# Rows of x ahead of a halved weight unit, half of the first values on another engine, scales in two bank pairs, two router rows shared by GpSimd and ScalarE

## The reference

```python
for i in range(DEPTH):                      # 2
    hn = rms_norm(h, norm_mix[i])
    if i % N_MIXERS == 0:                   # [B|C|h] = hn @ w_in; (B * conv3(C * h)) @ w_out
        h = h + short_conv_mixer(hn, conv_w_in[j], conv_w[j], conv_w_out[j])
    else:                                   # 3 head groups, (window, dilation) = (128,1), (512,4), (2048,16)
        h = h + dilated_attention_mixer(hn, attn_w_qkv[j], attn_w_o[j], cos, sin)
    hn = rms_norm(h, norm_ffn[i])           # top-1 of 4 groups, then top-2 of its 4 experts
    h = h + hierarchical_moe(hn, ...)       # silu(t @ w_gate[e]) * (t @ w_up[e]) @ w_down[e]
return rms_norm(h, norm_final)
```

## Time and profile before

| what | us |
| --- | --- |
| median of 3 runs (range) | 1403.17 (1402.56 to 1404.1) |
| the profiled execution | 1403.41 |
| its span, first to last instruction | 1401.6 |
| TensorE products busy | 1341.8 (96%) |
| VectorE busy | 1119.0 (80%) |
| ScalarE busy | 768.2 (55%) |
| GpSimd busy | 202.0 (14%) |

### The profile page before, as it was taken

One profiled execution on the slowest core, in us unless ns is written; L12 is line 12 of the kernel. 1 busy time (PEld: TensorE's weight loads), 2 busy tenths in 40 slices (PEclk: granted clock), 3 DMA queues, 4 the chain that ended last, 5 costly groups with the idle time before them and its releaser, 6 DMA issues.

```text
span 1401.6 us, 20107 instructions
## 1 busy us (share of the span) xinstructions
PE 1341.8 (96%) x6967; PEld 1104.2 (79%) x6967; DVE 1119.0 (80%) x1442; ACT 768.2 (55%) x946; POOL 202.0 (14%) x309
## 2 busy tenths in 40 slices
PE   7999988999999999999999999999997899999995
PEld 5888876888888877888888778888776788888883
DVE  6656368999999995994978768687967899999998
ACT  5222245888888856223357242224824588888882
POOL 3000021111111300221200111111002011111131
PEclk9999997999999999999999999999998899999998
DMA  5238417999999975232210222331035799999984
GB/s 211 91 121 309 188 61 260 359 389 390 392 397 388 379 268 176 83 121 90 90 61 2 99 97 92 106 103 61 2 122 207 261 378 387 392 382 394 388 341 180
DMA packets 85377, 308.92 MB, mean 220 GB/s; under 512 B 12177, under 2 KB 12201, under 8 KB 68932
## 3 DMA queue, kind: packets, MB, share of 16 engines
q1 hardware_dynamic: 75936, 291.19, 56.1%
q0 software_dynamic: 8640, 15.86, 3.0%
q10 hardware_dynamic: 740, 1.07, 0.2%
HBM read 291.72 MB, written 31.98 MB: 231 GB/s over the span
## 4 chain that ended last, share of the span: by engine, by line
PE 86%; DVE 7%; issue 3%; ACT 2%; DMA 1%; SPq 0%; DVEq 0%; POOLq 0%; ACTq 0%; POOL 0%
PE ps L329 26%; PE ps L331 25%; PE ps L330 25%; PE ps L1910 2%; PE ps L1695 2%; PE ps L1893 1%; DVE probT L1474 1%; PE ps L1590 1%; DVE h L1253 1%; PE ps L1875 1%; ACT v_all L927 1%; DVE rope_b L1541 1%; DMA x_rows<-hn_rows,tok_col 1%; DVE W_lo L978 1%; PE ps L1878 1%
## 5 line engine op out<-in xcount | busy, mean ns | idle before, releaser
L1179 DVE TENSOR_TENSOR W_lo<-m_raw,W_hi 128x2048 fp32r<-128x2048 f32 x192 | 435.9, 2290 | 48.7 <-ACT W_hi L738 48.1
L329 PE MATMUL ps<-W_hi,xT_hi_all 128*128 128x512 f32 x1024 | 408.7, 399 | 5.6 <-DVE xT_lo_all L1187 4.7
L331 PE MATMUL ps<-W_hi,xT_lo_all 128*128 128x512 f32 x1024 | 401.7, 392 | 0.0
L330 PE MATMUL ps<-W_lo,xT_hi_all 128*128 128x512 f32 x1024 | 400.5, 391 | 0.0
L738 ACT ACTIVATE W_hi<-m_raw 128x2048 fp32r<-128x2048 f32 x192 | 367.1, 1914 | 42.8 <-PE ps L331 42.2
L691 ACT ACTIVATE W_hi<-raw,mix_gain 128x512 fp32r<-128x512 f32 x192 | 122.9, 712 | 298.1 <-issue 283.2
L329 PEld LDWEIGHTS ps<-W_hi,xT_hi_all 128*128 128x128 f32 x1024 | 193.2, 189 | 50.1 <-DVE xT_lo_all L1187 5.1
L978 DVE SCALAR_TENSOR_TENSOR W_lo<-raw,mix_gain,W_hi 128x512 fp32r<-128x512 f32 x192 | 144.8, 815 | 106.0 <-ACT W_hi L691 105.6
L329 PE MATMUL ps<-xT_hi_all,W_hi 128*128 128x512 f32 x576 | 227.2, 394 | 1.9 <-DVE W_lo L978 1.9
L331 PEld LDWEIGHTS ps<-W_hi,xT_lo_all 128*128 128x128 f32 x1024 | 193.2, 189 | 42.2
L330 PE MATMUL ps<-xT_lo_all,W_hi 128*128 128x512 f32 x576 | 225.3, 391 | 0.0
(11 more groups left out here) (251 smaller groups left out, 1329.1 us busy)
## 6 DMA issues: line engine op xcount, KB each, us to landing
m_raw<-in_w_gate_dram SPq DMA_DIRECT2D x64, 1024.0 KB, 7.8
m_raw<-in_w_up_dram SPq DMA_DIRECT2D x64, 1024.0 KB, 9.1
m_raw<-in_w_down_dram SPq DMA_DIRECT2D x64, 1024.0 KB, 9.0
raw<-in_attn_w_qkv_dram SPq DMA_DIRECT2D x36, 1024.0 KB, 5.1
raw<-in_conv_w_in_dram SPq DMA_DIRECT2D x12, 1024.0 KB, 5.3
y_rows<-zero_rows SPq DMA_DIRECT2D x2, 4096.0 KB, 17.4
y_pick<-y_rows SPq DMA_DIRECT2D x16, 512.0 KB, 7.0
raw<-in_conv_w_out_dram SPq DMA_DIRECT2D x4, 1024.0 KB, 7.4
```

Of the source, the lines that this page charges most:

```text
L329: pe.matmul(o, a_hi, b_hi, start=first, stop=False)
L330: pe.matmul(o, a_hi, b_lo, start=False, stop=False)
L331: return pe.matmul(o, a_lo, b_hi, start=False, stop=last)
L1179: dve.tensor_tensor(MW_lo[c % MSPLIT][:, :, :], m_raw[c % MRAW][:, :, :], MW_hi[c % MSPLIT][:, :, :].bitcast(F), ALU.subtract).then_inc(s[ ...
```

## The change

**Start.** SyncE issues all four rows of x first, then the first weight unit as two DMAs of half the size. ScalarE takes the four rows, then the four pieces of the unit, the first two behind the first half. VectorE does the same with the low parts. TensorE's conv loop is written out, and the rstd transposes stand in the first pass only.

**Router.** VectorE scales rows 0 and 1 alone. GpSimd multiplies rows 2 and 3 of h by the gain, into `hn`, as soon as the buffer is free, and ScalarE then scales them by rstd in place; SyncE stores them behind ScalarE. VectorE copies the second row's logits before row 3's low part and makes `first_id`, a copy of `dest_id` in fp32r with each number twice. `first_oh` is fp32r, and its product has two columns.

```diff
--- before.py
+++ after.py
-        first_oh = at("first_oh", [P, NT, P], F, FG + 14 * KB)
+        first_oh = at("first_oh", [P, NT, P], FR, FG + 14 * KB)
+        first_id = temp("first_id", [P, NT, 2], FR)
...
+        def spread_bank(hb, s):
+
+            return 4 if s == 0 and hb % 2 else 6
...
                 sp.dma_start(h[:, r, :], x_v[:, r, :]).then_inc(x_in[r], 16)
-                if r == 0:
-                    conv_unit(0, 0)
+            sp.dma_start(raw[0][:, 0:2, :], w_in_v[:, 0:2, D:D + 512]).then_inc(first_half_in, 16)
+            sp.dma_start(raw[0][:, 2:4, :], w_in_v[:, 2:4, D:D + 512]).then_inc(raw_in[0], 16)
...
-                    sp.wait_ge(hn_ready, first + r + 1)
+                    if r < 2:
+                        sp.wait_ge(hn_ready, 2 * l + r + 1)
+                    else:
+                        sp.wait_ge(row_scaled, 2 * l + r - 1)
                     sp.dma_start(hn_dram[r * P:(r + 1) * P, :], hn[r % 2][:, :]).then_inc(hn_stored[r % 2], 16)
...
-                rstd_tiles(first)
+                rstd_tile(first, 0)
+                rstd_tile(first, 1)
                 pool.wait_ge(gain_in, 16 * (k + 1))
-                pool.wait_ge(hn_ready, 4 * l + 3)
-                pool.wait_ge(row_scaled, l + 1)
-                row = hn[1][:, :].rearrange("p (k q) -> p k q", k=KD)
-                pool.tensor_tensor(row, row, gain[:, :].rearrange("p (q k) -> p k q", k=KD), ALU.mult
-                                   ).then_inc(hn_ready, 1)
+                for r in range(2, NT):
+                    rstd_tile(first, r)
+                    pool.wait_ge(hn_stored[r % 2], 32 * l + 16)
+                    pool.tensor_tensor(hn[r % 2][:, :].rearrange("p (k q) -> p k q", k=KD),
+                                       h[:, r, :].rearrange("p (q k) -> p k q", k=KD),
+                                       gain[:, :].rearrange("p (q k) -> p k q", k=KD), ALU.mult
+                                       ).then_inc(row_gained, 1)
 
...
-                act.wait_ge(raw_in[uc % RAW], rev * 32 + (uc // RAW + 1) * 16)
+                if (uc, rev) == (0, 0):
+                    act.wait_ge(first_half_in, 16)
+                else:
+                    act.wait_ge(raw_in[uc % RAW], rev * 32 + (uc // RAW + 1) * 16)
...
+                        if (uc, rev, k) == (0, 0, 2):
+                            act.wait_ge(raw_in[0], 16)
...
-                act.wait_ge(rstd_ready, first + 4)
-                act.wait_ge(hn_stored[1], 32 * l + 16)
-                act.activation(hn[1][:, :].rearrange("p (k q) -> p q k", k=KD),
-                               h[:, 3, :].rearrange("p (q k) -> p q k", k=KD), ACT.Copy, scale=rstd[:, 3:4]
-                               ).then_inc(row_scaled, 1)
+                for r in range(2, NT):
+                    act.wait_ge(row_gained, 2 * l + r - 1)
+                    act.wait_ge(rstd_ready, first + r + 1)
+                    act.activation(hn[r % 2][:, :], hn[r % 2][:, :], ACT.Copy, scale=rstd[:, r:r + 1]
+                                   ).then_inc(row_scaled, 1)
...
+                def first_rows_hi(a):
+                    act.wait_ge(s["turned"], a + 1)
+                    act.activation(xT_hi_all[:, FIRST_X + a, :], ps[:, 2 + a, :], ACT.Copy).then_inc(s["xhi"], 1)
...
-                rows_hi(0, FIRST_X)
+                first_rows_hi(0)
+                first_rows_hi(1)
...
-            turn_hi(0, 0)
+            for r in range(NT):
+                turn_hi(0, r)
             hi(0)
-            for r in range(1, NT):
-                turn_hi(0, r)
...
-                            for r in range(NT):
+                            for r in range(2 if rev == 0 else NT):
...
-                norm_row(k, first, 2)
...
                 logits_copy(l, 0)
+                logits_copy(l, 1)
+                dve.tensor_copy(first_id[:, :, :], bc(dest_id[:, 0], 2))
                 turn_lo(stage, 3)
-                logits_copy(l, 1)
...
+                def first_rows_lo(a):
+                    dve.wait_ge(s["xhi"], a + 1)
+                    dve.tensor_tensor(xT_lo_all[:, FIRST_X + a, :], ps[:, 2 + a, :],
+                                      xT_hi_all[:, FIRST_X + a, :].bitcast(F), ALU.subtract).then_inc(s["xlo"], 1)
...
-                rows_lo(0, FIRST_X)
+                first_rows_lo(0)
+                first_rows_lo(1)
...
-            turn_lo(0, 0)
+            for r in range(NT):
+                turn_lo(0, r)
             lo(0)
-            for r in range(1, NT):
-                turn_lo(0, r)
...
-                dve.tensor_tensor(near, ps[:, 6, :], near, ALU.mult)
-                after(dve.tensor_tensor(far, ps[:, 7, :], far, ALU.mult))
+                bank = spread_bank(hb, s)
+                dve.tensor_tensor(near, ps[:, bank, :], near, ALU.mult)
+                after(dve.tensor_tensor(far, ps[:, bank + 1, :], far, ALU.mult))
...
+            def first_values():
+
+                dve.wait_ge(v_ready, 2)
+                for r in range(2, NT):
+                    wait_qkv(dve, 0, 0, r)
+                    for t in range(NT):
+                        ins = dve.tensor_scalar(v_all[32 * r:32 * r + 32, 0, t, :], ps[32 * t:32 * t + 32, r, :],
+                                                rstd[32 * t:32 * t + 32, r:r + 1], None, ALU.mult)
+                    ins.then_inc(v_ready, 1)
 
...
+                        if rev == 0 and p == 2:
+                            first_values()
...
-                    ins = pe.matmul(ps[:, 4, 0:1], first_oh[:, r, :], dest_id[:, 0, r:r + 1], start=(r == 0),
+                    ins = pe.matmul(ps[:, 4, 0:2], first_oh[:, r, :], first_id[:, r, :], start=(r == 0),
...
-                def turn_x(i):
+                def turn_x(i, halves=False):
...
+                        if halves and k == 3:
+                            ins.then_inc(s["turned"], 1)
...
-                turn_x(0)
-                pe.wait_ge(s["xlo"], 1)
+                turn_x(0, True)
                 for j in range(3):
+                    if j < 2:
+                        pe.wait_ge(s["xlo"], j + 1)
...
-            with pe.Fori(0, 2) as c:
+            for c in range(2):
...
-                        if uc == 0:
+                        if uc + c == 0:
...
-                n = s * 4 + hb
+                n = s * 4 + hb - (1 if s == 0 else 0)
                 pe.wait_ge(scales_copied, s + 1)
-                if n:
+                if n > 0:
                     pe.wait_ge(merged, n)
...
-                        ins = pe.matmul(ps[HD * hd:HD * hd + HD, 6 + far, :], parts_b[:, n:n + 1].to_broadcast([48, HD]),
+                        ins = pe.matmul(ps[HD * hd:HD * hd + HD, spread_bank(hb, s) + far, :], parts_b[:, n:n + 1].to_broadcast([48, HD]),
```

## The result

The changed kernel takes **1391.38 us** (median of 4 runs, 1391.09 to 1392.37) against 1402.87 us for the kernel before (4 runs, 1402.03 to 1404.1): ratio 0.9919, 95% interval 0.9906 to 0.9931. The profiled execution took 1391.36 us for a span of 1389.6 us, 12.0 us less span than before. The forecast was 1390.7 us, range 1387 to 1396.5. A second measurement (experiment 12) gave 1392.55; both lie in the range.

What follows compares the result with a forecast made beforehand. TensorE, holding 86% of the chain that ended last, was taken as the bound. Terms 0.8 + 0.9 + 3.9 + 3.8 + 1.7 + 1.6 = 12.7 us off 1403.4 gave 1390.7 us, range 1387 to 1396.5.

Steps and rivals of the forecast that it cites:

- `beats` at 0.5 us: Sign in both routers: this VectorE comparison, no longer held by GpSimd's multiply, takes near 0.5 us, winning 1.4 and 1.2.
- A: The forecast itself: all terms arrive, 1390.7 us, by its own bounds 1387.5 to 1393.5; chance 0.70.
- Start, 0.8: Kernel start: rows of x ahead of the first weights bring TensorE's first product sooner; 0.8 us, bounds -2.5 to +3.
- Conv loop, 0.9: Conv loop written out: the second pass drops rstd transposes that nobody reads; 0.9 us.
- Routers, 3.9 and 3.8: Routers 0 and 1: sooner logits, `beats`, `first_oh` product and halves, less the gather's loss; 3.9 and 3.8 us.
- rival C: VectorE gives gains back: start and first values bring less, a row multiply still overlaps `beats`; 1394.8 us, chance 0.12.
- The logits: Each router: TensorE's last logits start earlier because VectorE no longer scales row 2; 0.9 us, bounds 0.5 and 1.2.
- the halves: Each router: gathered rows turned and split in halves, so the first expert product starts sooner; 1.4 us, 1.0 to 1.6.
- The gather, -0.3 and -0.2: Routers 0 and 1: the gather runs closer behind two 1 MB weight loads; 0.3 and 0.2 us lost, bounds 0 to 1.
- First values, 1.7: First values: VectorE copies eight of ScalarE's 16 blocks, and TensorE's wait goes; 1.7 us, bounds 0.8 and 1.8.
- Bank pairs, 1.6: Spreads of the scales in two bank pairs: the third no longer waits for a merge; 1.6 us, bounds 1.2 and 1.7.
- Rival B: Routers: GpSimd starts row 3's multiply before the cast `first_id`, holding it; 2.9 us a router, 1396.5 us, chance 0.13.

Runs made afterwards that it cites:

- experiment 12: The changed kernel itself, word for word, measured a second time: 1392.55 us.
- experiment 6: The changed kernel with the start of the kernel before (row 0 of x, the whole first weight unit, rows 1 to 3): 1391.7 us.
- experiment 10: The changed kernel with TensorE's conv loop as a loop of two passes again, rstd transposes in both: 1393.21 us.
- experiment 1: The changed kernel with GpSimd's row multiply written with one strided operand, the output, in place of two strided inputs: 1392.68 us.
- experiment 2: The changed kernel without GpSimd's multiply of row 3 in both routers, so the stored row 3 is not the reference's: 1388.97 us.
- experiment 5: The kernel of experiment 1 with the cast `first_id` moved between the two copies of the logits: 1388.94 us.
- experiment 9: The changed kernel with the first gathered rows turned and split as a whole again, not in halves: 1395.49 us.
- experiment 3: The changed kernel with SyncE's load of the final norm's gain (0.5 MB) moved behind the weight loads of layer 1: 1390.96 us.
- experiment 7: The changed kernel with all 16 copies of the first values on ScalarE again, none on VectorE: 1394.11 us.
- experiment 8: The changed kernel with all spreads of the scales in banks 6 and 7 again, each waiting for the merge before it: 1394.99 us.

## Why the prediction was right

The time and the mechanism were right: the sum said 12.7 us, the profiled execution 12.0. Inside the sum two misses (the multiply, the gather of router 1) and two strokes of luck (the clock in the start, the end of router 1's low stretch) nearly cancelled. By the medians the gain was 11.5 and 10.6 us, so part of the hit is luck. Of the signs named, two did not come: `beats` at 0.5 us, and `tok_col` 2.8 us sooner behind the conv stage, which came 1.9 us sooner (at 209.87 us, 14.0 behind the last half row, 15.9 before). The bounds of A, 1387.5 to 1393.5, are narrower than the terms' own: the start's alone, at -2.5, would give 1394.0.

- **Start, 0.8.** The first product came at 16.13, in the forecast's 15.8 to 16.4. The trace shows 1.7 us behind the start, but 1.2 of it is clock, since 2.5 us fewer of products ran at the low level. A second execution of the same kernel stood 0.8 us later there: 0.4 by its first product and 0.3 by the clock. By the medians the order alone is worth at most 0.8 us of time (experiment 6). The clock was named as the larger unknown, rightly.
- **Conv loop, 0.9.** Right, 0.93 in the trace, and no price for written-out code (experiment 10).
- **Routers, 3.9 and 3.8.** The trace gives 3.2 and 1.9 up to the first expert product. The step that failed is GpSimd's multiply: taken at 2.85 us, allowed to 3.3, it took 3.83 to 4.09 us with two strided inputs and a third access with unit stride. The forecast put its end at 204.5 in the time of the kernel before, which is 201.9 in the changed one, where the conv stage ends 2.65 us sooner; it ended at 203.97, 2.1 late, and `beats` brought 0.4 and 0.2 in place of 1.4 and 1.2. The overlap of a row multiply with `beats` is what rival C named. Experiments 1, 2 and 5 show the cause: 2.4 us with one strided operand, `beats` 0.49 us where no multiply runs.
- The logits came 1.0 us sooner in each router (0.9 forecast), the halves 1.5 each, from the landing on (1.4 forecast; 1.6 by experiment 9), `first_oh` in fp32r 0.5 (its products took 1.02 us, 1.87 before).
- **The gather, -0.3 and -0.2.** 0.2 in router 0, right; 1.35 in router 1, outside the bound of 1. What was overlooked is that SyncE moved not two loads but three closer to it, the weight loads from 6.1 to 4.4 us: the final gain's half megabyte stands in the same queue (experiment 3).
- **First values, 1.7.** VectorE's eight copies took 0.76 us each (0.69 forecast), and the wait still went; together with the spread 3.6 of trace, 3.3 forecast. Experiment 7 gives the same wait of 1.7.
- **Bank pairs, 1.6.** The wait of 1.6 is shown (experiment 8).
- **Rival B** was given 0.13 and did not happen, but it was nearer than that, and the error in the multiply's length is what kept it away. With a first multiply of 2.85 us the second would have begun at about 198.9 (198.03, and the 0.87 us that lay between the two), the cast at 198.95: an estimate, and too close to call. With 2.42 us the cast was held (experiment 1).
- The end brought 0.7 us that no term held. The low stretch of router 1 ends 3.3 us behind the first expert product, 5.2 us in the kernel before; that this is the reason is read off the trace and not tested.

## What to carry to other kernels

Work handed to an idle engine has to be priced in the form in which it will run there (which operands are strided), and then looked at again for what it holds up meanwhile: here GpSimd's multiply held two VectorE operations between places in SBUF, `beats` and even a cast of 8 elements per partition, for its whole rest. Put such small operations where no GpSimd operation runs, and check by the trace that shortening one thing has not moved another in front of it. When loads move ahead of a transfer that somebody waits for, count all that stand in their queue.

## What the runs showed of the hardware

- A GpSimd multiply of 128x1024 f32: 2.38 to 2.42 us with one strided operand, the output; 2.85 with one strided input and in place; 3.83 to 4.09 with two strided inputs.
- VectorE's cast of 128x8 from SBUF to SBUF took 2.05 us beside a multiply that had begun 0.36 us sooner, 0.15 us without one; a subtraction of 128x1024 with one input in PSUM and one in SBUF took 1.21 us either way.
- One wait of 1.6 us in a busy stretch was followed by 3.4 us at half clock in one profile and by none in another. The length of the low stretches differed between two executions of one kernel by 3.4 us in two places, at a cost of 0.3 us each; filled with products, 3.4 us cost 1.7. The medians of this kernel in two measurements were 1391.38 and 1392.55, so a difference of about 1 us between two kernels of this length is not told by one measurement of each.
- The gather of the first rows took 4.2 to 5.0 us whether two loads of 1 MB were begun 4.9 to 8.9 us earlier or none was, and also with half a megabyte ahead of them where they were begun 6.1 us or more earlier. With the half megabyte and loads begun 4.4 to 4.7 us earlier it took 5.7 to 6.5.
- With TensorE's waits filled the clock stayed at 1.00 through both routers, and the time fell by only 1.1 to 1.3 us, because VectorE's low parts came next.
